# Row-wise products of a three-layer block in units of 512 columns over half the contraction, with row norms interleaved tile by tile

## The reference

```
def rms_norm(x, g):
    xf = x.astype(jnp.float32)
    y = xf * lax.rsqrt(jnp.mean(xf * xf, axis=-1, keepdims=True) + EPS)
...
    merged = jax.nn.sigmoid(g_a + b_merge[0]) * p_a + jax.nn.sigmoid(g_b + b_merge[1]) * p_b
    out = jnp.einsum('bsd,de->bse', merged, w_out.astype(merged.dtype))
    return x + rms_norm(out, norm_post_g)
```

```
def odd_layer(x, mem, norm_g, w_in, qk_g, b_f, mem_norm_g, w_mem_kv, w_out):
    h = rms_norm_2(x, norm_g)
    cq, ck, cv, cf, mq, z = split_cols(h @ w_in, ODD_SPLIT)
...
    y = jnp.concatenate([yc, ym], axis=-1) * jax.nn.silu(z)
    return x + y @ w_out
```

## Time and profile before

| | |
|---|---|
| median of 3 runs (lowest to highest) | 1241.16 us (1240.08 to 1243.57) |
| the profiled execution: its time / its span | 1238.32 us / 1236.5 us |
| PE, PEld busy | 96%, 81% of the span |
| DVE, ACT, POOL busy | 51%, 46%, 11% |
| mean granted TensorE clock | 0.993 |

### The profile page before, as it was taken

One profiled execution on the slowest core, in us unless ns is written; L12 is line 12 of the kernel. 1 busy time (PEld: TensorE's weight loads), 2 busy tenths in 40 slices (PEclk: granted clock), 3 DMA queues, 4 the chain that ended last, 5 costly groups with the idle time before them and its releaser, 6 DMA issues.

```text
span 1236.5 us, 17158 instructions
## 1 busy us (share of the span) xinstructions
PE 1186.5 (96%) x6930; PEld 1002.9 (81%) x6930; DVE 634.9 (51%) x1173; ACT 568.3 (46%) x1026; POOL 133.1 (11%) x146
## 2 busy tenths in 40 slices
PE   5999999999999999999998999899979999999998
PEld 4887888888976777788897889677978889877788
DVE  5485423688234534525537654886335564356631
ACT  4433421334334544533335565777225476466620
POOL 1000000000000000000000005432400000522522
PEclk9999999999999999999998999999989999999999
DMA  5323332233321121233524334112223233122221
GB/s 179 105 87 100 103 102 80 91 102 102 103 66 38 35 68 46 106 103 102 187 69 103 87 84 102 36 35 69 69 68 105 68 102 111 53 70 74 72 86 52
DMA packets 119047, 105.78 MB, mean 86 GB/s; under 512 B 17836, under 2 KB 115500, under 8 KB 118968
## 3 DMA queue, kind: packets, MB, share of 16 engines
q1 hardware_dynamic: 117320, 98.46, 26.1%
q10 hardware_dynamic: 1648, 6.23, 1.4%
HBM read 102.55 MB, written 2.12 MB: 85 GB/s over the span
## 4 chain that ended last, share of the span: by engine, by line
PE 91%; DVE 4%; ACT 3%; issue 1%; DMA 1%; SPq 0%; DVEq 0%; ACTq 0%
PE acc L1446 23%; PE acc L1448 23%; PE acc L1447 23%; PE acc L1756 3%; PE aux L1782 3%; PE aux L1770 3%; PE aux L1600 2%; PE aux L1446 2%; PE aux L1448 2%; PE aux L1447 2%; PE aux L1614 1%; ACT whi L596 1%; DVE wlo L934 1%; PE acc L1761 1%; PE aux L1664 0%
## 5 line engine op out<-in xcount | busy, mean ns | idle before, releaser
L1446 PE MATMUL acc<-ht_hi,whi 128*128 128x512 f32 x736 | 292.8, 398 | 8.4 <-DVE wlo L934 4.3
L1448 PE MATMUL acc<-ht_hi,wlo 128*128 128x512 f32 x736 | 287.2, 390 | 0.0
L1447 PE MATMUL acc<-ht_lo,whi 128*128 128x512 f32 x736 | 287.0, 390 | 0.0
L934 DVE TENSOR_TENSOR wlo<-raw,whi 128x2048 fp32r<-128x2048 f32 x71 | 163.4, 2303 | 148.7 <-ACT whi L596 148.7
L1446 PEld LDWEIGHTS acc<-ht_hi,whi 128*128 128x128 f32 x736 | 138.5, 188 | 39.4 <-DVE wlo L934 7.1
L596 ACT ACTIVATE whi<-raw 128x2048 fp32r<-128x2048 f32 x71 | 135.3, 1909 | 61.8 <-DMA raw<-o_w_mem_kv_dram 33.2
L1447 PEld LDWEIGHTS acc<-ht_lo,whi 128*128 128x128 f32 x736 | 138.7, 188 | 29.9 <-issue 1.9
L1448 PEld LDWEIGHTS acc<-ht_hi,wlo 128*128 128x128 f32 x736 | 138.5, 188 | 29.3
L542 POOL TENSOR_SCALAR whi<-raw 128x512 fp32r<-128x512 f32 x64 | 43.7, 682 | 1036.0 <-DMA raw<-e_w_in_dram 764.1
L1446 PE MATMUL acc<-whi,ht_hi 128*128 128x256 f32 x416 | 117.8, 283 | 0.0
L1447 PE MATMUL acc<-wlo,ht_hi 128*128 128x256 f32 x416 | 117.7, 283 | 0.0
(11 more groups left out here) (223 smaller groups left out, 1976.5 us busy)
## 6 DMA issues: line engine op xcount, KB each, us to landing
raw<-w_in_dram SPq DMA_DIRECT2D x72, 512.0 KB, 4.6
raw<-o_w_in_dram SPq DMA_DIRECT2D x28, 512.0 KB, 4.7
raw<-e_w_in_dram SPq DMA_DIRECT2D x18, 512.0 KB, 4.8
raw<-w_proj_pool_dram SPq DMA_DIRECT2D x8, 512.0 KB, 4.0
raw<-w_proj_mlstm_dram SPq DMA_DIRECT2D x8, 512.0 KB, 4.1
raw<-w_out_dram SPq DMA_DIRECT2D x8, 512.0 KB, 4.6
raw<-o_w_out_dram SPq DMA_DIRECT2D x8, 512.0 KB, 4.6
raw<-e_w_in_dram SPq DMA_DIRECT2D x12, 256.0 KB, 4.1
```

The costliest lines, as they stand in the source:

```text
L934: v.tensor_tensor(wlo[:, slot, :], raw[:, slot, :], whi[:, slot, :].bitcast(F32), ALU.subtract).then_inc(w_split, 1)
L1446: mm(out_, w_hi_, x_hi, start=first, stop=False)
L1447: mm(out_, w_hi_, x_lo, start=False, stop=False)
L1448: return mm(out_, w_lo_, x_hi, start=False, stop=last)
```

## The change

Of the row stages' 21 units, 20 (all but the third of `o_v`) are recut. A unit now holds 512 columns of 4 of the 8 contraction tiles, still 1 MB. Two units make one wide product of 512 columns: four row tiles, each in a bank of its own, so all four banks. `wide_rows` runs the first unit over all four row tiles, then the second, and each row tile is finished 12 matmuls after the one before. A slot is given back after the first unit through a new semaphore, `first_half_done`. In `out` stages two contraction tiles, then one, stand where three and three stood among the last attention steps.

Evacuation goes by row tile of 512 columns. In `wout` and `e_out` variances, roots, the new rows of `x`, and the next layer's norm are done per row tile within the last wide product. The memory's transposes come four and four; `memT` of the o layer lies elsewhere. At the layer changes PE's transposes of `xnrow` go by row tile around the memory unit's two halves; in the o layer `sum_squares` for the memory's keys moves behind the first unit of queries. The output goes to memory in four transfers instead of five.

```
+        WIDE = 2 * UC
+        WIDE_UNITS = {"v": 4, "wout": 4, "e_v": 2, "e_out": 4, "o_v": 2, "o_out": 4}
+        UNIT_DONE, FIRST_HALVES = [], {}
         for name, (n0, a0, units) in plan.items():
             for u in range(units):
-                UNIT_ACCS.append(a0 + 3 if name == "mix" else a0 + u)
+                if u < WIDE_UNITS.get(name, 0):
+                    if u % 2 == 0:
+                        FIRST_HALVES[n0 + u] = len(FIRST_HALVES) + 1
+                    UNIT_DONE.append(2 * (a0 + u + 1))
+                else:
+                    UNIT_DONE.append(2 * (a0 + 4 if name == "mix" else a0 + u + 1))
+
+        def wait_unit_done(eng, n):
+
+            if n in FIRST_HALVES:
+                eng.wait_ge(first_half_done, FIRST_HALVES[n])
+            else:
+                eng.wait_ge(acc_ready, UNIT_DONE[n])
+
+        def wide_bank(a, t):
+
+            return acc[:, 2 * ((a + t // 2) % 2) + t % 2, :]
...
+            def load_wide(view, col, n, kh):
+                slot_free(n)
+                for k in (0, 2):
+                    sp.dma_start(raw4[:, n % SLOTS, k:k + 2, :],
+                                 view[:, 4 * kh + k:4 * kh + k + 2, col:col + WIDE]).then_inc(w_loaded[n % SLOTS], 16)
+
+            def stage_wide(name, view, col0, units):
+                for u in range(units):
+                    load_wide(view, col0 + WIDE * (u // 2), plan[name][0] + u, u % 2)
...
-            heads_of_transposes("e_mem", memT[0][0], MEM)
 
             n0, a0, units = plan["wout"]
-            for u in range(units):
-                for t in range(TT):
-                    act.wait_ge(acc_ready, 2 * (a0 + u) + 1 + t // 2)
-                    bank = acc[:, 2 * ((a0 + u) % 2) + t // 2, :]
-                    c = UC * (t % 2)
-                    nc.scalar.activation(junk[:, UC * t:UC * t + UC], bank[:, c:c + UC], ACT.Square,
-                                         accum_out=stats[:, 5, units * t + u:units * t + u + 1]).then_inc(post_ssq, 1)
-                act.wait_ge(post_ssq, TT * (u + 1))
-                weight_heads(n0 + u + 2)
-            act.wait_ge(post_var, 1)
-            nc.scalar.activation(small[:, 0:4], small[:, 0:4], ACT.Sqrt).then_inc(post_sd, 1)
+
+            def post_square(c, t):
+                act.wait_ge(acc_ready, 2 * a0 + 4 * c + t + 1)
+                if c:
+                    act.wait_ge(post_ssq, t + 1)
+                nc.scalar.activation(junk[:, t, :], wide_bank(a0, t), ACT.Square,
+                                     accum_out=stats[:, 5, 2 * t + c:2 * t + c + 1]).then_inc(post_ssq, 1)
+
+            def row_square(t, rows):
+                act.wait_ge(x_rows, rows)
+                nc.scalar.activation(xnrow[:, t, :], xrow[:, t, :], ACT.Square,
+                                     accum_out=small[:, t:t + 1]).then_inc(rssq_ready, 1)
+            weight_heads(n0 + 3)
+            for t in range(TT):
+                post_square(0, t)
+            heads_of_transposes("e_mem", memT[0][0], MEM, tiles=range(4))
+            weight_heads(n0 + 4)
+            heads_of_transposes("e_mem", memT[0][0], MEM, tiles=range(4, KT))
+            for t in range(TT):
+                post_square(1, t)
+                act.wait_ge(post_var, t + 1)
+                nc.scalar.activation(small[:, t:t + 1], small[:, t:t + 1], ACT.Sqrt).then_inc(post_sd, 1)
+                if t:
+                    row_square(t - 1, t)
+                    root(t - 1)
+                if t == 2:
+                    weight_heads(n0 + 5)
+            row_square(3, TT)
+            root(3)
...
-                squares(xrow, xnrow, TT, 0,
-                        lambda t: act.wait_ge(*((x_rows, t + 1) if L == 0 else (acc_free, plan["e_out"][1] + 4))))
                 if L:
-                    for half in range(2):
-                        head_norm_squares(a0, half, MEM)
+                    for t in range(TT):
+                        row_square(t, TT + t + 1)
+                        root(t)
+                        if t == 1:
+                            weight_heads(plan["o_mem"][0] + 1)
+                for half in range(2):
+                    head_norm_squares(a0, half, MEM)
                 if L == 0:
                     weight_heads(plan["e_qk"][0])
-                heads_of_transposes(name + "_norm", ht_hi, S)
+                heads_of_transposes(name + "_norm", ht_hi, S, tiles=range(4))
+                value_rows(a0 + 1, mv, MT, 0)
+                heads_of_transposes(name + "_norm", ht_hi, S, tiles=range(4, KT))
                 weight_heads(plan[name + "_qk"][0] + 1)
-                value_rows(a0 + 1, mv, MT, 0)
                 head_norm_rsqrt(MEM)
...
                     squares(memrow, memn, MT, 20, lambda t: act.wait_ge(mem_in, 32))
+                    heads_of_transposes("o_mem", memT[1][0], MEM, tiles=range(4))
                     weight_heads(plan["o_mem"][0])
-                    heads_of_transposes("o_mem", memT[1][0], MEM)
-                    weight_heads(plan["o_mem"][0] + 1)
+                    heads_of_transposes("o_mem", memT[1][0], MEM, tiles=range(4, KT))
...
+            for t in range(TT):
+                var = small[:, t:t + 1]
+                dve.wait_ge(post_ssq, TT + t + 1)
+                step(v.tensor_tensor(var, stats[:, 5, 2 * t:2 * t + 1], stats[:, 5, 2 * t + 1:2 * t + 2], ALU.add))
+                v.tensor_scalar(var, var, 1.0 / D, EPS, ALU.mult, ALU.add).then_inc(post_var, 1)
+                gain(1, t)
+                dve.wait_ge(post_sd, t + 1)
+                if t % 2:
+                    dve.wait_ge(acc_free, a0 + 3 + t // 2)
+                step(v.reciprocal(small[:, 4 + t:5 + t], var))
                 v.scalar_tensor_tensor(xrow[:, t, :], orow1[:, t, :], small[:, 4 + t:5 + t], xagain[:, t, :],
                                        ALU.mult, ALU.add).then_inc(x_rows, 1)
-            weight_rests(n0 + units + 1)
+                if t:
+                    row_variance(t - 1, 0)
+                    scale_rows(xrow, xnrow, t - 1, 0)
+                if t == 2:
+                    weight_rests(n0 + 5)
+            row_variance(3, 0)
+            scale_rows(xrow, xnrow, 3, 0)
...
+                def residual(c, t):
+                    a = a0 + 2 * c
+                    dve.wait_ge(acc_ready, 2 * a + t + 1)
+                    rows = xrow[:, t, WIDE * c:WIDE * c + WIDE]
+                    ins = v.tensor_tensor(rows, wide_bank(a, t), rows, ALU.add)
+                    if t % 2:
+                        ins.then_inc(acc_free, 1)
+                    elif c and L == 0:
+                        ins.then_inc(x_rows, 1)
+                    elif c and t == 2:
+                        ins.then_inc(last_rows, 1)
+                    if t % 2 and c and L == 0:
+                        dve.wait_ge(acc_free, a + t // 2 + 1)
+                        dve.sem_inc(x_rows, 1)
+                for t in range(TT):
+                    residual(0, t)
+                if L == 0:
+                    rests_of_transposes("o_mem", *memT[1], MEM, tiles=range(4))
+                    weight_rests(plan["o_mem"][0])
+                    rests_of_transposes("o_mem", *memT[1], MEM, tiles=range(4, KT))
+                for t in range(TT):
+                    residual(1, t)
+                    if L == 0 and t:
+                        row_variance(t - 1, 0)
+                        scale_rows(xrow, xnrow, t - 1, 0)
+                    if L == 0 and t == 2:
                         weight_rests(plan["o_mem"][0] + 1)
+                if L == 0:
+                    row_variance(3, 0)
+                    scale_rows(xrow, xnrow, 3, 0)
...
+            def wide_product(n, a, t, k, x_hi, x_lo):
+
+                s, c = n % SLOTS, WIDE * (k % 4)
+                return product(wide_bank(a, t), x_hi[:, k, P * t:P * t + P], x_lo[:, k, P * t:P * t + P],
+                               whi[:, s, c:c + WIDE], wlo[:, s, c:c + WIDE], k == 0, k == KT - 1)
+
+            def wide_rows(n, a, x_hi, x_lo, between=None):
+
+                for kh in range(2):
+                    wait_split(pe, n + kh)
+                    for t in range(TT):
+                        if kh == 0 and t % 2 == 0:
+                            pe.wait_ge(acc_free, a + t // 2 - 1)
+                        for k in range(4 * kh, 4 * kh + 4):
+                            ins = wide_product(n + kh, a, t, k, x_hi, x_lo)
+                        if kh:
+                            ins.then_inc(acc_ready, 1)
+                    if kh == 0:
+                        ins.then_inc(first_half_done, 1)
+                        if between is not None:
+                            between()
+
+            def rows_as_tiles_come(n, a, x_hi, x_lo, rests_before, tiles):
+
+
+
                 for k in tiles:
+                    if k == 0:
+                        pe.wait_ge(acc_free, a)
+                    if k % 4 == 0:
+                        wait_split(pe, n + k // 4)
```

(37 more changed lines are left out.)

256 lines of the change are left out of this document (111 added, 145 removed).

## The result

The changed kernel takes 1219.78 us (median of 4 runs, 1218.48 to 1222.94) against 1240.62 us before (4 runs, 1238.99 to 1243.57): ratio 0.983, 95% interval 0.981 to 0.986. It is faster by 20.8 us. The forecast was 1212.0 with a range of 1206.5 to 1218.5: the sign was right and the size was not, and the median lies 1.3 us above the range. A repetition beside other runs gave 1220.39 us, ratio 0.983 (0.980 to 0.985). One execution in the slow state (the kernel of experiment 4, 1682.04 us at a mean granted clock of 0.655) is in no median.

A forecast was written before the change was run, and what follows sets the result against it. PE, busy for 96% of the span, was taken to bound the kernel. The terms 12.2 + 1.2 + 5.2 + 9.6 + 2.0 - 1.0 gave 29.2 us less, median 1241.16 to 1212.0 us, range 1206.5 to 1218.5.

The forecast's parts named there:

- Item 1: Row stages: 960 matmuls of 512 columns replace pairs of 256, 12.7 ns saved each, 12.2 us less on PE's path.
- Item 2: Borders inside a stage: banks and weight loads come in time for wide products, so nothing gained or lost.
- Items 3: `wout`: the memory's transposes come four and four with free bank pairs; 1.2 us less.
- item 5: `e_out`: memory transposes no longer all stand behind ACT's `whi` of `o_mem`, which waits for its load; 9.6 us less.
- 6: Start of both `out` stages: the wait for the last gated tile goes; 1.0 us each, 2.0 us together.
- Item 4: Change to the e layer: 28.7 us against 33.84, 5.2 us less, with a 2.8 us wait for DVE's norm of tile 2.
- Item 7: Change to the o layer: a new wait of 2.2 us before the third unit of queries; 48.0 against 46.95, 1.0 us more.
- the rival with a fall: Clock falls in item 4's new wait of 2.8 us; four to five us at half clock lose 2.4: 1214.4 us; chance 0.17.
- The first rival: The same rival: clock falls in item 4's new wait, losing 2.4 us, 1214.4 us; chance 0.17.
- item 8: `v`, `e_v`, `o_v` and the tail: nothing beyond the width gain of item 1.
- The rival that gave 1219: DVE and ACT later at layer changes than reckoned: item 4 gains nothing, item 7 loses 2 more; 1219 us; chance 0.13.

The follow-up runs named there:

- experiment 4: The changed kernel with POOL starting its third `e_z` unit only when eight pairs of the e attention are done: 1218.66 us, ratio 0.982.
- experiment 7: The changed kernel with the first contraction tile of a wide product waiting for its banks in pairs, not all four at once: 1220.18 us.
- experiment 8: The changed kernel with `wout`'s variances, roots, rows of `x` and row norm put back behind the last piece: 1223.80 us.

## Why the prediction was right or wrong

Item 1, the width: right. 226.7 ns where 119.7 twice stood, in `v`, `wout`, `e_v` and `e_out` alike. The rule of the Trainium skill that the prediction sets against this item ("TensorE: Matmul & The Clock Gate", section "Back-to-back issue gap") would have given 2.4 us in all. `v` alone gained 2.5: the measurement decides against it for this stream.

Item 2, borders at nothing: right inside the stages, wrong at the first border. I had asked when the banks of a second wide product come free, and not that the first tile of `wout` asks for all four where the unit before gives two: 0.9 us (experiment 7).

Items 3, 5 and 6: right. `wout` 45.51 (45.3), `e_out` 47.18 (47), `o_out` 3.2 us shorter (3.4). Of item 5 most of its cause was shown too, with 8.0 of 9.6 us by the order alone. (60.23 less 46.0 is 14.2 and not 14.3; nothing hangs on it.)

Item 4: right, 29.16 us (28.7), wait 2.97 (2.8). That was luck, an execution without a fall there. In all six others with this order and these norms it fell, and then the stretch takes 30.5 to 31.8 us and the gain is 2.0 to 3.4 us. Of work alone the gain is an estimated 1.9 us of the 4.7, 31.1 to 29.2 (experiment 8); the greater part was the clock.

Item 7: the mechanism right, its terms off in both ways. The stretch to the third unit took 48.36 us (48.0), the wait was 1.47 and 0.30 us, not 2.2. What it set off, a fall, was in no term; the rival with a fall spoke of item 4's wait alone.

**The step that failed** is the sum's term for the clock. The sum took the profiled execution of before, took away two waits with the half clock behind them (items 4 and 5), and kept the clock whole all over the rest. Of the 29.2 us, 4.9 were this half clock by the estimate above. They came, and four falls at other places took some 6.5 us back: 6.5 of the 9.6 us that are missing. A profile with no fall behind a wait of 2.00 us I read as a rule that such a wait is harmless; it was one throw, and behind the same wait the clock fell in 7 of 13. The thirteen profiles lost 3.4 to 10.2 us of clock to falls, now here, now there. The first rival had the right mechanism, but gave it one place and 2.4 us, where some seven places each can have one.

The work came short too, 21.2 us of 24.3 (19.6 and the 6.5, less the 4.9). Two parts have a cause that was shown: the 0.9 us of item 2, and the e attention, which no item names (item 8 has only `v`, `e_v`, `o_v` and the tail) and the sum so left at nothing. It had a stall behind POOL that stood in the trace of before as three unexplained waits, 0.90, 1.91 and 1.70 us. I had asked whether POOL's work moves in the row stages, and not what it does to DVE where it moves. It moved by 1.5 us against the logits, PE waited 0.9 us more, and the clock fell behind the longest wait. The last 1.3 us are terms of 0.1 to 0.5 us that weren't traced.

The rival that gave 1219, close to the median, was wrong in its cause: DVE's norm came at T+9.8 where T+9.3 was reckoned, and items 4 and 7 came within 0.5 us.

## What to carry to other kernels

Sum a forecast from stretches with the clock whole, count the waits that can make it fall, and add these as an expected number for each kernel; one trace shows one throw. Count as won only the half clock that lies behind a wait, not the part inside it. Where a transfer or a slot moves, look at what POOL does beside DVE's instructions on the critical path: an addition of 256 numbers that takes 1.1 us is not slow, it stands. Before a stage is rebuilt for a long wait, look at what stands ahead in the list of the engine that is waited for: one moved line gave 6.4 us, where the whole change gave 20.8.

## What the runs showed of the hardware

- Whether the clock falls behind a wait of 1.5 to 2.3 us differs between executions: behind the 2.00 us in `mix`, in code that is the same in all thirteen profiles, 7 times of 13. Behind 39 equal waits of 1.84 us in heads 1 to 3 it never fell, and I can't say why. A fall is 1.7 us of clock and cost 1.5 to 1.7 us of time, less where part of it lay inside the wait. Two came together behind every wait of 4.6, 6.1 and 7.0 to 7.1 us, and behind one of the seven of 2.97 us.
- An addition of 128 by 2 numbers on DVE, both inputs in SBUF, that starts while POOL runs an instruction with two inputs ends with it. In the profiles before and after all eight of this kind ended 15 to 17 ns after POOL's; they took 0.37 to 1.27 us in place of 0.16.
- With the granted clock equal, most stretches of tens of microseconds repeat to 0.1 us between executions, so single profiles tell differences of 0.2 us in a stretch that medians of four runs don't tell. The e attention is an exception: behind the same code the wait for `zT` at 776 us was 2.33 to 3.58 us.
